# Splitting each modulation product around the column halves of its network product

## The chip, the cores and the metric

The kernel runs on one core of one Trainium2 chip. The time is device microseconds of one execution on that core. Three runs of the kernel before gave 2127.76, 2130.54 and 2132.85 us; the median is 2130.54 us.

## The reference

Two blocks of a model run one behind the other on 256 tokens of width 1024. The first block has two layers; each ends with a convolutional gated network (hidden width 2816):

```python
def conv_glu(x, w_in, conv_w, conv_b, w_out):
    gate, val = jnp.split(x @ w_in, 2, axis=-1)
    gate = lax.conv_general_dilated(gate, conv_w[:, None, :], ...) + conv_b   # 3 taps along the tokens
    return (jax.nn.gelu(gate, approximate=False) * val) @ w_out
```

The second block needs modulation vectors that do not depend on x:

```python
def ada_params(sc, w, b):          # sc: silu of the condition, w: 1024 x 6144, for each of two layers
    mod = sc @ w + b
    return [t[:, None, :] for t in jnp.split(mod, 6, axis=-1)]
```

The kernel computes layer 0's modulation product inside the first convolutional stage and layer 1's inside the second, because sc (two rows: context and latent) is known from the start. Everything else of the reference (attention, state-space mixer, conformer module, gated networks) lies outside the change.

## The kernel before

**Slabs.** All weights come as slabs of 128 x 2048 fp32 (1 MB), in one fixed order, into a ring of four places in SBUF. SyncE issues every load in that order, one queue, one behind the other. Before the load of slab g it waits for one of two things (L2235 to L2240 of `sync`): as a rule for the semaphore `slab_begun` to reach g - 2, which TensorE counts up when it begins a slab's product, so that the slab four places earlier is done with; for most network slabs of the convolutional stages it waits instead for `lo_ready`, since those slabs are no longer read once they are split.

**Splitting.** A network slab isn't multiplied as it lies in the ring. ScalarE copies it into `w_hi` (fp32r, `hi`, L2696, two halves of 128 x 1024), GpSimd writes the rest ring - w_hi as a second fp32r tile (`lo`, L2146, two halves). In the stages f0 and f1 the rest goes to the place of `w_hi` before its own, so that only two networks are held at a time: ScalarE may write network n+2 only once network n's product is done (`one_conv` waits for `full["dve"][u]` and then calls `ahead`). TensorE computes three matmuls for each of 8 row chunks and 2 column halves: w_hi by x_hi (L1664), rest by x_hi (L1666), w_hi by x_lo (L1668). That makes 48 matmuls for one network, 24 for a column half `ch`.

**The two stages.** f0 and f1 have 46 slabs each: modulation slab 0, network slab 0, modulation slab 1, network slab 1 and so on up to 21, and then modulation slabs 22 and 23. In program order TensorE does modulation product u (`ada`, L1885: 8 fp32 matmuls, each in the trace as two records; the output is 32 partitions wide, so four of them stand side by side in the 128 partitions of one bank, and the second four are summed onto the first), and then network product u (`col_T_split`). A loop of five rounds does four pairs each, two pairs follow, then the last two modulation products and the second product of the network (`rows_split`, L1718, eleven slabs "fo").

**Who frees what.** `begun` raises `slab_begun` by 2 on the first matmul of the network product: once for the modulation slab just used, once for the network slab. One further count was given just before the stage. So the load of modulation slab n+2, which takes the place of modulation slab n, goes out when network n begins, and network slab n+2 is the next one in SyncE's queue; its own wait, for the rest of network n, is over by then. The first two slabs of the second product, fo0 and fo1, go out in the same way when network 21 begins.

```python
# TensorE, network(layer)
with L.rounds(5, per | {("took", "lo_ready"): 8}) as i:
    for u in range(4):
        ada(stage, 2 * u, u, 2 * i)
        col_T_split(stage, 2 * u + 1, u, waits=turned if u == 0 else None)
# SyncE
for g in range(SLABS):
    if g in halves_read:
        sp.wait_ge(S["lo_ready"], halves_read[g])
    elif g >= RING:
        sp.wait_ge(S["slab_begun"], g - 2)
    sp.dma_start(ring[:, g % RING, :], slabs[SOURCE[g]]).then_inc(landed[g % RING], 16)
```

**Behind the products.** VectorE turns each modulation result (`turn_ada`, L2358) and then works on the network (`convolved`, L2338 to L2350), with ScalarE's gelu and copies in between. Two banks serve the modulation products, four the networks.

Of the kernel before, what the change touches and what calls it, by code (L numbers as in the profile page):

```python
# [34 lines left out]
KC = D // P  # L35
# [142 lines left out]
def build(nc, slabs, x_in, xT_in, memT_in, ctx_in, pt_in, row_in, ln_in, wdt_in, out):  # L178
    with ExitStack() as ctx:
# [113 lines left out]
        def part(name, at, *dims):  # L293
            return nc.alloc_sbuf_tensor_at(name, [P, *dims], F32R, offset=at)
# [3 lines left out]
        x_hi = part("x_hi", arena_at + 4 * 18432, KC, T)  # L298
        x_lo = part("x_lo", tri_at, KC, T)
# [1277 lines left out]
        def _(pe):  # L1577
# [3 lines left out]
            def free_of(b):  # L1581

                return free[last.get(b, "act")][b]

            def frees(b):

                return L.now((last.get(b, "act"), b))
# [3 lines left out]
            def fill(ins, b, first, then=None):  # L1591

                ins.then_inc(full[first][b], 1)
                if first == "dve":
                    filled_dve[b] += 1 if L.per is None else 5
                last[b] = then or first
                L.up((last[b], b))

            def for_rounds(reader):

                for b in range(4):
                    if last[b] != reader:
                        pe.wait_ge(free_of(b), frees(b))
                        last[b] = reader

            def slab(stage, u, i=0):

                g = FIRST[stage] + u
                pe.wait_ge(landed[g % RING], 16 * (g // RING + 1) + i * 16)
                return ring[:, g % RING, :]  # L1610

            def begun(ins, first, slabs=1):

                if first and slabs:
                    ins.then_inc(S["slab_begun"], slabs)
# [25 lines left out]
            def pair(stage, u):  # L1644

                pe.wait_ge(S["lo_ready"], L.took("lo_ready", 2))
                return (FIRST[stage] + u) % RING

            def col_T_half(stage, u, ch, b, src=(x_hi, x_lo), used_up=False, waits=None):

                if ch == 0:
                    pair(stage, u)
                    pe.wait_ge(free_of(b), frees(b))
                s = (FIRST[stage] + u) % RING
                wh = w_hi[:, s, :].rearrange("p (k c) -> p k c", k=KC)
                early = stage in ("f0", "f1")
                wl = (w_hi[:, (s - 1) % RING, :] if early else w_lo[:, s, :]) \
                    .rearrange("p (k c) -> p k c", k=KC)
                dst, c = bank[b][:, ch * T:(ch + 1) * T], slice(ch * P, (ch + 1) * P)
                for k in range(KC):  # L1660
                    if waits and ch == 0 and k in waits:
                        for sem, count in waits[k]:
                            pe.wait_ge(sem, count)
                    ins = pe.matmul(dst, wh[:, k, c], src[0][:, k, :], start=(k == 0), stop=False)  # L1664
                    begun(ins, ch == 0 and k == 0, 2 if early else 1)
                    ins = pe.matmul(dst, wl[:, k, c], src[0][:, k, :], start=False, stop=False)  # L1666
                    begun(ins, used_up and ch == 1 and k == KC - 1)
                    ins = pe.matmul(dst, wh[:, k, c], src[1][:, k, :], start=False,  # L1668
                                    stop=(k == KC - 1))
                if ch == 1:  # L1670
                    fill(ins, b, "dve" if early else "act")

            def col_T_split(stage, u, b, src=(x_hi, x_lo), used_up=False, waits=None):

                for ch in range(2):
                    col_T_half(stage, u, ch, b, src, used_up, waits)

            def turned_x():

                return {0: [(free_of(b), frees(b)) for b in (4, 6)],  # L1680
                        4: [(free_of(b), frees(b)) for b in (5, 7)]}
# [189 lines left out]
                        fill(ins, 4 + q, "act")  # L1871
                    marks["ctxT"] = {b: L.now(("act", b)) for b in range(8)}

            def ada(stage, u, r, i=0, last_one=False):

                w = slab(stage, u, i).rearrange("p (k c) -> p k c", k=KC)  # L1880
                b = 5 + r % 2
                pe.wait_ge(free_of(b), frees(b))
                for k in range(KC):
                    q = 32 * (k % 4)
                    ins = pe.matmul(bank[b][q:q + 32, 0:256], sc_in[:, k, :], w[:, k, :],  # L1885
                                    start=(k < 4), stop=(k >= 4))

                    begun(ins, k == 0 and last_one)
                fill(ins, b, "dve")

            def ada_columns(layer):

# [9 lines left out]
            def network(layer):  # L1902

                stage = f"f{layer}"
                if layer == 0:
                    pe.wait_ge(S["sc_ready"], L.took("sc_ready"))
                    pe.wait_ge(S["pick_ready"], L.took("pick_ready"))
                for_rounds("dve")
                marks[f"net{layer}"] = dict(filled_dve)
                marks[f"ada{layer}"] = {b: L.now(("dve", b)) for b in (0, 1, 2, 3, 5, 6)}  # L1910
                turned = turned_x()
                for b_ in (5, 6):
                    pe.wait_ge(free_of(b_), frees(b_))
                    last[b_] = "dve"
                per = {("dve", q): 1 for q in range(4)} | {("dve", q): 2 for q in (5, 6)}
                with L.rounds(5, per | {("took", "lo_ready"): 8}) as i:
                    for u in range(4):

                        ada(stage, 2 * u, u, 2 * i)
                        col_T_split(stage, 2 * u + 1, u, waits=turned if u == 0 else None)  # L1920
                for u in range(2):
                    ada(stage, 2 * u, u, 10)
                    col_T_split(stage, 2 * u + 41, u)
                ada(stage, 4, 2, 10)
                ada(stage, 5, 3, 10, last_one=True)
                def between(j):

                    if j == 2:
                        ada_columns(layer)
                    if layer:  # L1930
                        turn_ctx(j)
                rows_split(f"fo{layer}", hook=between)
# [25 lines left out]
            for h in range(DIFF_HEADS + 3):  # L1958
                if h < DIFF_HEADS:
                    for c in range(2):  # L1960
                        b = 4 + 2 * (h % 2) + c
                        pe.wait_ge(free_of(b), frees(b))
                    for tt in range(NT):
                        for c in range(2):
                            part = slice(c * HEAD, (c + 1) * HEAD)
                            ins = pe.matmul(bank[4 + 2 * (h % 2) + c][:, tt * T:(tt + 1) * T],
                                            qT[part, h, tt * P:(tt + 1) * P], kT[part, h, :],
                                            start=True, stop=True)
                            if tt:
                                fill(ins, 4 + 2 * (h % 2) + c, "dve")  # L1970
                if h >= 3:
# [3 lines left out]
                    for tt in range(NT):  # L1975
                        for kt in range(NT):
                            ins = pe.matmul(bank[2][:, tt * P:(tt + 1) * P],
                                            aT[:, g % 2, kt * T + tt * P:kt * T + (tt + 1) * P],
                                            vN[:, kt, g * P:(g + 1) * P],
                                            start=(kt == 0), stop=(kt == NT - 1))  # L1980
                    fill(ins, 2, "act")
                if 0 <= h - 2 < DIFF_HEADS:
# [3 lines left out]
                    for kt in range(NT):  # L1986
                        for tt in range(NT):
                            ins = pe.transpose(bank[g % 2][:, kt * T + tt * P:kt * T + (tt + 1) * P],
                                               aS[:, g % 3, tt * T + kt * P:tt * T + (kt + 1) * P],
                                               ident[:, :])  # L1990
                    fill(ins, g % 2, "act")
                if h < DIFF_HEADS:
                    col_T_half("xk0", h // 2, h % 2, 3, (m_hi, m_lo))
                else:
                    for g in (2 * (h - 8), 2 * (h - 8) + 1):
                        turn_head(g)
# [3 lines left out]
            cross(0)  # L2000
            while_norm("T", "xk1", used_up=True)
            network(0)
            tokens_to_T(by_class=True)
            turned = turned_x()
# [23 lines left out]
            for q in range(pairs + 3):  # L2028
                if q < pairs:
                    for tt in range(NT):  # L2030
# [3 lines left out]
                        for g, (at, n, cols) in enumerate([(0, T, slice(0, T)), (T, P, keys),  # L2034
                                                           (T + P, P, keys)]):
                            for hh in range(2):
                                part = slice(hh * HEAD, (hh + 1) * HEAD)
                                ins = pe.matmul(bank[2 * hh + tt][:, at:at + n],  # L2038
                                                gqT[part, 8 * g + q, tt * P:(tt + 1) * P],
                                                gkT[part, 8 * g + q, cols], start=True, stop=True)  # L2040
# [4 lines left out]
                if q >= 3:  # L2045
                    k = q - 3
                    b = 6 + k % 2
# [6 lines left out]
                    for n, (g, kt, cols) in enumerate(blocks):  # L2054
                        wide = cols.stop - cols.start
                        for hh in range(2):
                            col = g * D + (2 * k + hh) * HEAD
                            ins = pe.matmul(bank[b][hh * HEAD:(hh + 1) * HEAD, cols],
                                            gvN[:, kt, col:col + HEAD],
                                            gPT[:, 2 * (k % 2) + hh, at:at + wide],  # L2060
                                            start=(n == 0), stop=(n == 5))
# [932 lines left out]
```

## Time and profile before

| what | value |
|---|---|
| median of 3 runs | 2130.54 us |
| the profiled execution, its own time | 2126.64 us |
| span of the profiled execution | 2124.9 us |
| PE busy | 1931.2 us (91%) |
| POOL busy | 1258.8 us (59%) |
| DVE busy | 1083.8 us (51%) |
| ACT busy | 994.5 us (47%) |

The span is the profiled part of the one execution; the other 1.7 us of its time lie around it. PE is TensorE's matmuls, PEld its weight loads, DVE VectorE, ACT ScalarE, POOL GpSimd, SPq the queue of SyncE. Busy time of PE includes pipelining: a matmul of 256 columns has a record of about 0.28 us, but in a stream the next one starts 0.12 us later. So the start times say how fast a stream runs, and the busy share does not. The two convolutional stages lie at about 302 to 463 us and 940 to 1104 us of the span.

### The profile page before, as it was taken

The page shows a single profiled execution, that of the slowest core. Times are in us where ns is not written, and L with a number is a line of the kernel's source. Part 1 is how long each engine was busy: PE and PEld are TensorE (multiplying, and loading weights), DVE is VectorE, ACT ScalarE, POOL GpSimd, SP SyncE. Part 2 cuts the span into 40 slices and gives each one's busy share as a digit, 9 for nine tenths or more (in the row PEclk, how much of TensorE's full clock was granted, in tenths as well). Part 3 has the DMA queues.
Part 4 walks back from the last instruction along what each step waited for, and adds up shares of the span by engine and source line. Part 5 has one row for each costly group of instructions (what it writes and reads, how often), then busy time and mean ns, then how long its engine had stood idle before and what let it go on. Part 6 is the DMA issues. An engine that isn't in the chain of part 4 may idle for free.

```text
span 2124.9 us, 33890 instructions
## 1 busy us (share of the span) xinstructions
PE 1931.2 (91%) x13581; PEld 1704.6 (80%) x13581; DVE 1083.8 (51%) x1511; ACT 994.5 (47%) x1718; POOL 1258.8 (59%) x588
## 2 busy tenths in 40 slices
PE   6879989999899979989999889998879998978997
PEld 6868888877899966868877868876669987948996
DVE  7783146641100073136657655678767942846641
ACT  3453435443444373434554444478744546425542
POOL 9647566678688602646669334300468885426995
PEclk9999999999899999999999999999989998989999
DMA  6325367764555503357774212211235553314552
GB/s 251 139 93 186 112 224 293 302 259 175 177 181 190 187 1 139 119 220 279 298 274 161 80 62 97 99 60 64 86 135 182 181 194 121 119 61 164 182 192 104
DMA packets 48321, 342.30 MB, mean 161 GB/s; under 512 B 5264, under 2 KB 6288, under 8 KB 7248
## 3 DMA queue, kind: packets, MB, share of 16 engines
q1 hardware_dynamic: 45968, 328.22, 42.3%
q0 software_dynamic: 2240, 12.49, 1.5%
q8 instruction: 80, 1.31, 0.2%
q14 instruction: 33, 0.27, 0.0%
HBM read 339.65 MB, written 1.05 MB: 160 GB/s over the span
## 4 chain that ended last, share of the span: by engine, by line
PE 65%; DVE 17%; ACT 7%; POOL 5%; issue 5%; DMA 1%; DVEq 0%; POOLq 0%; SPq 0%; ACTq 0%
PE bank L1664 11%; PE bank L1668 11%; PE bank L1666 11%; PE bank L1718 11%; DVE arena L902 2%; POOL w_lo L2146 2%; PE bank L1762 2%; PE bank L1277 2%; POOL w_hi L2146 2%; PE bank L1279 2%; PE bank L1280 2%; PE bank L1699 2%; PE bank L1698 2%; PE bank L1696 2%; ACT arena L1102 2%
## 5 line engine op out<-in xcount | busy, mean ns | idle before, releaser
L2146 POOL TENSOR_TENSOR w_lo<-ring,w_hi 128x1024 fp32r<-128x1024 f32 x360 | 876.8, 2461 | 314.4 <-ACT w_hi L2696 313.9
L1664 PE MATMUL bank<-x_hi,w_hi 128*128 128x256 f32 x2176 | 615.7, 283 | 29.9 <-POOL w_lo L2146 16.6
L1668 PE MATMUL bank<-x_lo,w_hi 128*128 128x256 f32 x2176 | 618.4, 284 | 0.0
L2696 ACT ACTIVATE w_hi<-ring 128x1024 fp32r<-128x1024 f32 x448 | 448.7, 1052 | 348.8 <-DMA ring<-slabs_dram 344.7
L1664 PEld LDWEIGHTS bank<-x_hi,w_hi 128*128 128x128 f32 x2176 | 414.4, 190 | 50.5 <-issue 50.5
L1668 PEld LDWEIGHTS bank<-x_lo,w_hi 128*128 128x128 f32 x2176 | 413.6, 190 | 0.0
L1666 PE MATMUL bank<-x_hi,w_lo 128*128 128x256 f32 x1472 | 413.4, 281 | 0.0
L1666 PEld LDWEIGHTS bank<-x_hi,w_lo 128*128 128x128 f32 x1472 | 281.3, 191 | 0.0
L2146 POOL TENSOR_TENSOR w_hi<-ring,w_hi 128x1024 fp32r<-128x1024 f32 x88 | 208.8, 2394 | 110.9 <-ACT w_hi L2696 110.9
L2634 ACT ACTIVATE arena<-bank 128x512 f32<-128x512 f32 (+1 forms) x182 | 100.1, 563 | 296.9 <-PE bank L1668 190.8
L1666 PE MATMUL bank<-x_hi,w_hi 128*128 128x256 f32 x704 | 197.5, 281 | 0.0
L398 POOL TENSOR_TENSOR w_lo<-ring,w_half 128x1024 fp32r<-128x1024 f32 x32 | 77.7, 2433 | 112.3 <-ACT w_half L989 112.2
L1666 PEld LDWEIGHTS bank<-x_hi,w_hi 128*128 128x128 f32 x704 | 132.9, 189 | 0.0
L2594 DVE CUSTOM_DVE_ANT_0 arena<-bank,dist 128x512 f32<-128x512 f32 x32 | 22.1, 692 | 214.9 <-PE bank L2038 214.3
L1718 PE MATMUL bank<-w_hi,h_hi 128*128 128x512 f32 x352 | 112.9, 398 | 11.4 <-POOL w_lo L2146 9.8
L711 DVE SCALAR_TENSOR_TENSOR arena<-bank,pt,arena 128x508 f32<-128x508 f32 (+3 forms) x128 | 87.3, 682 | 60.0 <-ACT arena L1004 56.4
L1718 PE MATMUL bank<-w_lo,h_hi 128*128 128x512 f32 x352 | 112.1, 396 | 0.0
L1718 PE MATMUL bank<-w_hi,h_lo 128*128 128x512 f32 x352 | 111.9, 395 | 0.0
L1277 PE MATMUL bank<-s_hi,w_half 128*128 128x512 f32 (+1 forms) x288 | 104.6, 363 | 2.0 <-DVE s_lo L643 2.0
L2350 DVE TENSOR_TENSOR h_lo<-arena,h_hi 128x256 f32 (+1 forms) x44 | 85.2, 1936 | 33.3 <-ACT h_hi L2778 33.3
L1280 PE MATMUL bank<-s_hi,w_lo 128*128 128x512 f32 (+1 forms) x288 | 101.9, 354 | 0.0
L1279 PE MATMUL bank<-s_lo,w_half 128*128 128x512 f32 (+1 forms) x288 | 101.8, 353 | 0.0
(341 smaller groups left out, 3657.9 us busy)
## 6 DMA issues: line engine op xcount, KB each, us to landing
ring<-slabs_dram SPq DMA_DIRECT2D x312, 1024.0 KB, 4.8
lnrow<-ln_dram POOLq DMA_DIRECT2D x6, 1024.0 KB, 5.0
xt<-xT_dram SPq DMA_DIRECT2D x1, 1024.0 KB, 5.9
xt<-memT_dram POOLq DMA_DIRECT2D x1, 1024.0 KB, 14.0
x<-x_dram POOLq DMA_DIRECT2D x1, 1024.0 KB, 17.9
arena<-ctx_dram POOLq DMA_DIRECT2D x1, 1024.0 KB, 7.0
lnrow<-ln_dram POOLq DMA_DIRECT2D x2, 512.0 KB, 4.8
res<-x POOLq DMA_DIRECT2D x2, 512.0 KB, 3.2
```

What stands on the lines that cost most here:

```text
L711: ins = v.scalar_tensor_tensor(out=d3[:, :, lo:hi], in0=s3[:, :, lo + o:hi + o], scalar=pt[:, scw + k * 32 + j:scw + k * 32 + j + 1], in1= ...
L1277: ins = pe.matmul(dst, wh[:, k, :], hi_(k), start=(k == 0), stop=False)
L1279: pe.matmul(dst, wh[:, k, :], lo_(k), start=False, stop=False)
L1280: ins = pe.matmul(dst, wl[:, k, :], hi_(k), start=False, stop=(k == KC - 1))
L1664: ins = pe.matmul(dst, wh[:, k, c], src[0][:, k, :], start=(k == 0), stop=False)
L1666: ins = pe.matmul(dst, wl[:, k, c], src[0][:, k, :], start=False, stop=False)
L1668: ins = pe.matmul(dst, wh[:, k, c], src[1][:, k, :], start=False, stop=(k == KC - 1))
L1718: ins = pe.matmul(bank[2 * tt + h][:, :], st, w[:, k, h * 512:(h + 1) * 512], start=(first and n == 0), stop=(end and n == 2))
L2146: pool.tensor_tensor(dst[:, c], ring[:, s, c], w_hi[:, s, c].bitcast(F32), ALU.subtract).then_inc(S["lo_ready"], 1)
L2350: v.tensor_tensor(h_lo[:, j, :], act[:, u, :], h_hi[:, j, :].bitcast(F32), ALU.subtract).then_inc(S["hT_ready"], 1)
L2634: a.activation(dst, bank[b][:, :] if src is None else src, ACT.Copy if not kw else ACT.Identity, **kw).then_inc(free["act"][b], 1)
L2696: a.activation(w_hi[:, g % RING, c], ring[:, g % RING, c], ACT.Copy) \
```

## The change

Each pair of a modulation product and its network product becomes: four modulation matmuls (k = 0 to 3), the first column half of the network, the other four modulation matmuls (k = 4 to 7), the second column half. The modulation slab is then in use until the middle of the network, so the count of 2 on `slab_begun` moves from the first matmul of column half 0 to the first matmul of column half 1. All instructions stay; one wait on the landed slab is added for each pair. The last two modulation products stay whole.

```diff
@@ col_T_half
                     ins = pe.matmul(dst, wh[:, k, c], src[0][:, k, :], start=(k == 0), stop=False)
-                    begun(ins, ch == 0 and k == 0, 2 if early else 1)
+                    if early:
+                        begun(ins, ch == 1 and k == 0, 2)
+                    else:
+                        begun(ins, ch == 0 and k == 0)
@@ col_T_split
-            def col_T_split(stage, u, b, src=(x_hi, x_lo), used_up=False, waits=None):
+            def col_T_split(stage, u, b, src=(x_hi, x_lo), used_up=False, waits=None, between=None):
                 for ch in range(2):
+                    if ch and between:
+                        between()
                     col_T_half(stage, u, ch, b, src, used_up, waits)
@@ ada
-            def ada(stage, u, r, i=0, last_one=False):
+            def ada(stage, u, r, i=0, last_one=False, half=None):
                 w = slab(stage, u, i).rearrange("p (k c) -> p k c", k=KC)
                 b = 5 + r % 2
-                pe.wait_ge(free_of(b), frees(b))
-                for k in range(KC):
+                if half != 1:
+                    pe.wait_ge(free_of(b), frees(b))
+                for k in range(KC) if half is None else range(4 * half, 4 * half + 4):
                     q = 32 * (k % 4)
                     ins = pe.matmul(bank[b][q:q + 32, 0:256], sc_in[:, k, :], w[:, k, :],
                                     start=(k < 4), stop=(k >= 4))
                     begun(ins, k == 0 and last_one)
-                fill(ins, b, "dve")
+                if half != 0:
+                    fill(ins, b, "dve")
+
+            def ada_and_net(stage, j, u, i=0, waits=None):
+                ada(stage, 2 * j, u, i, half=0)
+                col_T_split(stage, 2 * j + 1, u, waits=waits,
+                            between=lambda: ada(stage, 2 * j, u, i, half=1))
@@ network
                     for u in range(4):
-                        ada(stage, 2 * u, u, 2 * i)
-                        col_T_split(stage, 2 * u + 1, u, waits=turned if u == 0 else None)
+                        ada_and_net(stage, u, u, 2 * i, turned if u == 0 else None)
                 for u in range(2):
-                    ada(stage, 2 * u, u, 10)
-                    col_T_split(stage, 2 * u + 41, u)
+                    ada_and_net(stage, 20 + u, u)
```

## Rows read from the trace of the kernel before

**Rows 1.** Page: the span, and TensorE's busy time, share and instructions.

```profile
span 2124.9 us, 33890 instructions
PE 1931.2 (91%) x13581; PEld 1704.6 (80%) x13581; DVE 1083.8 (51%) x1511; ACT 994.5 (47%) x1718; POOL 1258.8 (59%) x588
```

**Rows 2.** Windows, network 1 to 21, both stages: span, PE, PEld, DVE, ACT, POOL, PEclk, DMA, GB/s.

```profile
311.87:450.53 138.66, 137.37 (x1280) 122.71 (x1281) 88.49 (x116) 69.29 (x109) 95.00 (x40) 1.00 0.79 303
949.45:1092.16 142.71, 137.48 (x1285) 122.74 (x1281) 87.03 (x118) 69.90 (x110) 94.86 (x40) 1.00 0.77 298
```

**Rows 3.** Waits, 300 to 460 us: us in total, times, longest.

```profile
ACT w_hi L2696 <- DMA ring<-slabs_dram: 52.7, 21, 4.2
POOL w_hi L2146 <- ACT w_hi L2696: 50.2, 21, 6.5
```

**Rows 4.** Waits of SyncE's queue, 300 to 460 us.

```profile
SPq L2240 <- PE bank L1664: 131.7, 22, 7.6
```

**Rows 5.** Timeline, network 11 and its successors: start, us, engine, line [idle before <-releaser].

```profile
380.29 0.28 PE L1668 MATMUL bank<-x_lo,w_hi 128*128 128x256 f32 x1
380.50 1.07 PE L1885 MATMUL bank<-ring,sc_in 128*32 128x256 f32 x16
381.54 0.19 PEld L1664 LDWEIGHTS bank<-x_hi,w_hi 128*128 128x128 f32 x1 [0.45 <-issue]
381.57 0.36 PE L1664 MATMUL bank<-x_hi,w_hi 128*128 128x256 f32 x1
...
381.95 0.33 SPq L2240 DMA_DIRECT2D ring<-slabs_dram  x1
382.32 0.43 SPq L2240 DMA_DIRECT2D ring<-slabs_dram  x1
...
387.18 0.28 PE L1668 MATMUL bank<-x_lo,w_hi 128*128 128x256 f32 x1
...
389.26 2.01 ACT L2696 ACTIVATE w_hi<-ring 128x1024 fp32r<-128x1024 f32 x2 [3.41 <-DMA ring<-slabs_dram]
390.40 4.74 POOL L2146 TENSOR_TENSOR w_hi<-ring,w_hi 128x1024 fp32r<-128x1024 f32 x2 [2.21 <-ACT w_hi L2696]
...
395.37 0.38 PE L1664 MATMUL bank<-x_hi,w_hi 128*128 128x256 f32 x1
```

**Rows 6.** The tile sc_in: records of the modulation products, ns min/median/max.

```profile
L1885 PE MATMUL bank<-ring,sc_in x768: 379/379/637, 302.4 to 1099.6; 128*32 128x256 f32 x192
```

**Rows 7.** Line L2240, the loads issued at 381.95 and at 382.32 us.

```profile
DMA to landing us min/median/max: 4.8/4.8/4.8
...
DMA to landing us min/median/max: 6.9/6.9/6.9
```

**Rows 8.** Timeline, first stage: start of network 1, of network 21, and fo0's way to TensorE.

```profile
311.87 0.36 PE L1664 MATMUL bank<-x_hi,w_hi 128*128 128x256 f32 x1 [1.56 <-issue]
...
450.53 0.36 PE L1664 MATMUL bank<-x_hi,w_hi 128*128 128x256 f32 x1
...
456.47 2.01 ACT L2696 ACTIVATE w_hi<-ring 128x1024 fp32r<-128x1024 f32 x2 [1.99 <-PE bank L1668]
...
462.63 0.76 PE L1718 MATMUL bank<-w_hi,h_hi 128*128 128x512 f32 x1 [4.33 <-POOL w_lo L2146]
```

**Rows 9.** Timeline, second stage: network 0, network 2's copy, starts of networks 2, 3, 21.

```profile
941.97 0.58 PE L1664 MATMUL bank<-x_hi,w_hi 128*128 128x256 f32 x1
...
952.81 2.01 ACT L2696 ACTIVATE w_hi<-ring 128x1024 fp32r<-128x1024 f32 x2 [2.90 <-DMA ring<-slabs_dram]
...
958.89 0.36 PE L1664 MATMUL bank<-x_hi,w_hi 128*128 128x256 f32 x1 [2.51 <-POOL w_hi L2146]
...
965.71 0.39 PE L1664 MATMUL bank<-x_hi,w_hi 128*128 128x256 f32 x1
...
1092.15 0.39 PE L1664 MATMUL bank<-x_hi,w_hi 128*128 128x256 f32 x1
```

**Rows 10.** Windows of two waits of TensorE, columns as in rows 2.

```profile
956.00:958.00 2.00, 0.37 (x8) 0.00 (x0) 0.58 (x2) 1.27 (x5) 2.00 (x2) 1.00 0.25 102
...
462.00:464.00 2.00, 1.37 (x3) 1.16 (x4) 0.00 (x0) 2.00 (x3) 1.96 (x2) 0.53 0.01 4
```

## The prediction

> **What bounds the kernel now.** I read the page first, then the two stages that the change touches by windows, then their waits, and last the timeline of one pair. On the page [rows 1] TensorE is busy for 91% of the span; the reader is to see from it only that a delay of TensorE will seldom be hidden. It doesn't say what paces the stages. The windows [rows 2] take twenty pairs each: 138.66 us in the first stage, 142.71 us in the second, so 6.93 and 7.14 us for one pair, with the granted clock at 1.00. The waits [rows 3] show a second pace beside TensorE's: ScalarE waits 52.7 us in 21 places for a slab to land, and GpSimd 50.2 us for ScalarE. SyncE itself waits 131.7 us, 22 times, for the first matmul of a network, L1664 [rows 4]. So the loads aren't ahead of their use; each goes out on a signal from TensorE.
>
> The timeline of one pair [rows 5] puts both paces side by side. TensorE alone: the last matmul of network 10 starts at 380.29, the block of 16 modulation records at 380.50, network 11 at 381.57, its last matmul at 387.18. That is 1.28 us across the block, then 5.61 us for 47 steps, 0.119 us each: 6.9 us for a pair. The chain of one slab: network 11 begins at 381.57; its signal lets the load of modulation slab 13 go at 381.95 and that of network slab 13 at 382.32, 0.75 us after the start. ScalarE starts on it at 389.26, 6.94 us after the issue; the landing times, 4.8 us for the first of the two loads and 6.9 us for the second, agree [rows 7]. GpSimd starts at 390.40 (1.14 us more) and needs 4.74 us, to 395.14. Network 13 begins at 395.37, 0.23 us later. The sum is 0.75 + 6.94 + 1.14 + 4.74 + 0.23 = 13.8 us for two pairs, exactly two times 6.9. TensorE's own work and the way from its signal back to it are equal here. Whatever makes the signal later, by d, adds d to every second pair, with no slack in between.
>
> **The change, part by part.** Removed: nothing. *The mid-network half.* The block of eight matmuls is four groups of four; the whole takes 1.07 us and one record 0.38 us [rows 5, 6], so the groups follow at (1.07 - 0.38) / 3 = 0.23 us. Across a whole block I read 1.28 us from matmul to matmul; across half of one I take 1.28 - 2 x 0.23 = 0.82 us, which assumes that entering (0.21 us) and leaving (0.45 us from the last modulation weights to the first network weights, rows 5) cost the same as now. The trace has no such half block. From below its cost is the two groups alone, 0.46 us (plus one step of 0.12), from above the whole block, 1.28 us. I take 0.82, because the gaps on either side belong to the change of shape and stay whole for a half. TensorE's own work for a pair becomes 46 x 0.119 + 2 x 0.82 = 7.1 us, 0.2 us more than now.
>
> The row shows weights of the network waiting 0.45 us behind the modulation records [rows 5]. The Trainium skill ("TensorEngine Tiling (Array Packing)", Tiling Modes, Key Properties) says that changing the tiling mode drains the engine; by that rule the change pays two drains more for each pair, which is the 0.82 taken here, and the row agrees. Another of its pages ("TensorE: Matmul & The Clock Gate", Part 3) has TensorE pull weight loads ahead of running matmuls where groups differ; by that one the half would cost 0.46 us and the total below would be some 8 us less. The row speaks against it.
>
> *The moved signal.* It moves from the first matmul of column half 0 to that of column half 1: 23 steps of 0.119 and the half block, 2.74 + 0.82 = 3.6 us after the start of the network. Both loads move with it. The modulation slab waits for the signal itself, and the network slab is queued behind it on SyncE, though its own condition (the rest of network n is written) has long been met. Behind them come ScalarE's copy, and behind that in ScalarE's order the gelu, and GpSimd's rest; TensorE waits for the last. The chain for two pairs is now 13.8 + 3.6 = 17.4 us, 8.7 us a pair, against 7.1 us of TensorE's work. The cover that hid the load until now, the second and first halves of two networks, is used up, and TensorE will stand still for 1.6 us in each pair.
>
> *The rest* costs nothing: the wait on a landed slab in the middle is for a slab already in use; half a block less in front of the network falls into TensorE's new wait for GpSimd; VectorE turns a modulation result later, but its bank is asked for again two pairs on; VectorE's and ScalarE's work for one network (88.49 and 69.29 us in 20 pairs, rows 2) fits into 8.7 us; network 1's own slab is loaded before the first moved signal.
>
> *First stage.* From network 1 [rows 8] to 21 are ten double steps: 10 x 17.4 = 174.0 instead of 450.53 - 311.87 = 138.66 us: +35.4. Then fo0, the first slab of the next product, is issued on network 21's signal. Now it has landed when network 21 ends, and ScalarE starts on it at 456.47, 5.94 us after the start of network 21. After, it is issued at 3.6 + 0.38 and lands 4.8 us later, at 8.8 us, and ScalarE takes it up at about 8.9: +3.0. From fo0 on TensorE paces the product, and the shift stays. Together +38.4 us.
>
> *Second stage.* The chain of the even networks begins at 941.97, on the slow clock and with a slow load: ScalarE gets network slab 2 at 952.81 [rows 9], where 0.75 + 6.94 would give 949.7. That excess is other traffic, which runs out meanwhile. After, I place the second issue near 947.0 and the landing at 954.0; so network 2 begins at about 960.1 (958.89 now), and network 3, whose load follows network 1's signal, at 967.1 (965.71 now): +1.4. From 3 to 21 are nine double steps: 967.1 + 9 x 17.4 = 1123.7 against 1092.15: +31.5. With +3.0 for fo0: +34.5 us.
>
> The sum is +73 us on the profiled execution's 2126.64 us: 2199.6 us. The median of the runs stands 3.9 us, or 0.2%, above that execution, so I predict 2203.5 us, 3.4% more.
>
> **The rivals.** *(A) The load is hidden anyway,* and only TensorE's changes of shape count. For it: the DMA engines are only busy 0.79 of the time [rows 2]. Against it: ScalarE already waits for the landing in 21 of 22 networks [rows 3], and the chain adds up to the whole double step. It would give 0.2 us x 44 pairs = +9 (up to 0.5 x 44 = +20 with the half at its dearest), about 2140 to 2150 us.
>
> *(B) The clock falls too.* TensorE now stands still in each pair. At 462 to 464, behind a wait of 4.3 us [rows 8], the granted clock was 0.53 [rows 10]. If each first column half ran at 1.2 GHz, its 23 steps and the half block would take some 2.7 us more in the chain (256 columns at 1.2 GHz are 0.213 us, against 0.119), 1.35 us a pair: +54 us on top with the tails, about 2258 us. Against it: around 956 to 958, with 0.37 us of matmuls in the 2 us and TensorE's next start only at 958.89, the clock stayed at 1.00 [rows 9, 10], and the new waits are shorter.
>
> *(C) Not slower: the half slips under the network's matmuls.* If four narrow matmuls in the middle cost one group's pitch and no change of shape (0.23 + 0.12 us, twice a pair), TensorE's pair would be 46 x 0.119 + 0.7 = 6.2 us, 0.7 us under today's, and with the landing free of the signal up to 44 x 0.7 = 31 us would be gained, 2100 us. It decides only from where the chain gets below 13.8 us. Even at 0.35 us the signal is 3.1 us later, so the landing would have to come 3.8 us after the issue, and the shortest in the rows is 4.8 us, for the first of the two loads [rows 7]. I see nothing that speaks for this.
>
> **How the numbers follow.** The forecast gets 0.8, (A) 0.07, (B) 0.08, (C) 0.03, and 0.02 remain for something else. The forecast's own range: the half block at 0.46 or 1.28 us moves nineteen double steps and two tails by -0.36 or +0.46 each, -8 or +10 us; the landing and the start behind GpSimd scatter by 0.1 to 0.2 us a step, 3 us; the second stage's beginning is open by some 3 us. That gives 2191 to 2217 us. To hold 8 in 10 the range has to be wider than that toward both neighbours, without reaching them: 2184 to 2232 us. A difference under 0.2% can't be told from none here. Slower by more than that hold the forecast, (A) and (B): 0.95 or so; faster 0.03, same 0.02.
>
> **What would show it.** In the changed kernel a double step between networks should be 17.4 us; the issues of SyncE 3.9 us behind the start of a network instead of 0.38; ScalarE's wait for the landing in each pair up from 2.5 us on average to about 5 us; TensorE's wait on GpSimd (L2146) near 1.6 us in each pair, 60 to 70 us in all; the landing still 6.9 us behind the issue; the clock still 1.00 in both stages; nothing moved outside them but the two tails. A double step near 14.3 us would make (A) right; a granted clock under 1.00 in the first halves, (B). The forecast is wrong if the signal isn't what the loads wait for, or if the landing gets shorter than 6 us when it is alone.

## The result, and the profile after

The changed kernel takes 2227.54 us (median of 4 runs, 2222.74 to 2232.32), the kernel before 2129.15 us in the same comparison: ratio 1.0467, 95% interval 1.045 to 1.0483. It is slower by 98 us; the forecast was slower by 73 us, and the range (to 2232 us) holds the time. The profiled execution of the changed kernel took 2229.16 us.

The page of the changed kernel, the lines that answer to [rows 1], and the clock by slices:

```profile
span 2227.4 us, 33875 instructions
PE 1976.5 (89%) x13581; PEld 1730.8 (78%) x13581; DVE 1044.0 (47%) x1511; ACT 993.7 (45%) x1718; POOL 1255.3 (56%) x588
...
PEclk9999999999899999988999999999998999989999
```

The number of matmuls is the same, and the busy time of ScalarE and GpSimd too. The span grew by 102.5 us and TensorE's busy time by 45 us. Windows of the changed kernel, networks 1 to 21 of both stages, columns as in [rows 2]:

```profile
311.79:496.16 184.37, 153.62 (x1281) 130.14 (x1281) 88.76 (x117) 68.97 (x109) 94.19 (x40) 0.94 0.60 232
1001.85:1191.05 189.20, 160.36 (x1285) 136.29 (x1281) 90.78 (x121) 69.71 (x110) 94.17 (x40) 0.90 0.57 222
```

184.37 us against 138.66 us and 189.20 against 142.71 [rows 2]. The reader is to see two things: the DMA engines fell from 0.79 to 0.60 busy, so nothing new competes with the loads, they only start later, and the granted clock is 0.94 and 0.90, where it was 1.00. (While the loads of a pair run, the engines are full all the same: 0.96 to 1.01 at 392 to 394 and at 398 to 402, in the windows below.) From the start of network 0 in the second stage (941.97 us before, 993.53 us after) to fo0's product (1104.27 and 1206.07 us) the growth is 50.2 us; the first stage with its tail, to 462.63 and 513.38 us, grew by 50.8 us. All the rest of the kernel has 1.5 us more. The forecast had +34.5 us for the second stage and +38.4 us for the first.

Waits of the changed kernel in the first stage, 300 to 510 us, the lines that answer to [rows 3] and [rows 4] and the new one of TensorE:

```profile
ACT w_hi L2703 <- DMA ring<-slabs_dram: 113.5, 22, 9.9
POOL w_hi L2153 <- ACT w_hi L2703: 97.9, 21, 8.7
...
PE bank L1664 <- POOL w_hi L2153: 32.1, 12, 4.2
```

```profile
SPq L2247 <- PE bank L1664: 183.6, 22, 12.8
```

The timeline of the changed kernel around networks 6, 7 and 8, columns as in [rows 5], and the landing of the two loads issued there, as in [rows 7]:

```profile
356.29 0.39 PE L1664 MATMUL bank<-x_hi,w_hi 128*128 128x256 f32 x1
...
359.32 0.64 PE L1887 MATMUL bank<-ring,sc_in 128*32 128x256 f32 x8
359.89 0.19 PEld L1664 LDWEIGHTS bank<-x_hi,w_hi 128*128 128x128 f32 x1 [0.41 <-issue]
359.89 0.39 PE L1664 MATMUL bank<-x_hi,w_hi 128*128 128x256 f32 x1
...
360.11 0.28 PE L1669 MATMUL bank<-x_hi,w_hi 128*128 128x256 f32 x1
...
360.31 0.80 SPq L2247 DMA_DIRECT2D ring<-slabs_dram  x2
...
366.33 0.39 PE L1664 MATMUL bank<-x_hi,w_hi 128*128 128x256 f32 x1 [2.77 <-POOL w_hi L2153]
...
367.51 2.01 ACT L2703 ACTIVATE w_hi<-ring 128x1024 fp32r<-128x1024 f32 x2 [3.69 <-DMA ring<-slabs_dram]
...
373.62 0.35 PE L1664 MATMUL bank<-x_hi,w_hi 128*128 128x256 f32 x1
```

```profile
L2247 SPq DMA_DIRECT2D ring<-slabs_dram x2: 327/380/432, 360.3 to 360.7; - x2
...
DMA to landing us min/median/max: 4.7/5.8/6.8
```

Network 6 starts at 356.29, its column half 1 at 359.89: 3.60 us, as forecast. The loads go out at 360.31, ScalarE starts at 367.51, network 8 at 373.62: 17.3 us for the double step (from a network's start to that of the next but one), where 17.4 was forecast. So far every term holds. But the networks aren't evenly spaced. Network 7 starts 10.04 us after network 6, behind a wait of 2.77 us, and network 8 only 7.29 us after network 7. Two networks further on, in front of network 9, such a wait has a second effect (networks 9, 10 and 11, columns as in [rows 5], then the windows):

```profile
383.55 0.39 PE L1664 MATMUL bank<-x_hi,w_hi 128*128 128x256 f32 x1 [2.71 <-POOL w_hi L2153]
...
388.66 0.38 PE L1664 MATMUL bank<-x_hi,w_hi 128*128 128x256 f32 x1
...
391.47 0.28 PE L1671 MATMUL bank<-x_lo,w_hi 128*128 128x256 f32 x1
391.68 0.64 PE L1887 MATMUL bank<-ring,sc_in 128*32 128x256 f32 x8
392.25 0.39 PE L1664 MATMUL bank<-x_hi,w_hi 128*128 128x256 f32 x1
...
398.67 0.28 PE L1671 MATMUL bank<-x_lo,w_hi 128*128 128x256 f32 x1
398.88 0.64 PE L1887 MATMUL bank<-ring,sc_in 128*32 128x256 f32 x8
402.31 0.58 PE L1664 MATMUL bank<-x_hi,w_hi 128*128 128x256 f32 x1 [2.79 <-POOL w_hi L2153]
```

```profile
384.00:386.00 2.00, 2.00 (x16) 2.00 (x15) 1.18 (x3) 1.03 (x2) 0.00 (x0) 0.77 0.07 29
386.00:388.00 2.00, 2.00 (x13) 1.73 (x16) 0.78 (x2) 1.98 (x3) 1.90 (x1) 0.50 0.00 0
388.00:390.00 2.00, 2.00 (x19) 1.34 (x12) 0.43 (x2) 1.21 (x4) 2.00 (x2) 0.88 0.00 0
...
392.00:394.00 2.00, 2.00 (x22) 1.75 (x15) 1.51 (x3) 0.00 (x0) 0.00 (x0) 1.00 1.01 426
...
398.00:400.00 2.00, 1.51 (x16) 0.90 (x15) 0.42 (x1) 1.26 (x4) 2.00 (x2) 1.00 0.96 406
400.00:402.00 2.00, 0.00 (x0) 0.00 (x0) 1.97 (x1) 0.00 (x0) 2.00 (x1) 1.00 0.99 418
402.00:404.00 2.00, 1.69 (x8) 1.70 (x9) 1.53 (x3) 0.46 (x1) 0.25 (x1) 0.53 0.42 176
```

Behind the wait TensorE is on 1.2 GHz for part of the network (granted 0.50 and 0.53 of 2.4 GHz). Network 9's first half takes 5.11 us (383.55 to 388.66) instead of 3.60. So network 10, which comes behind it, starts 1.5 us later, and so does the signal for network 11. Since both are late by the same time, the wait in front of network 11 is as long as before, 2.79 us, and the clock is slow again. The median double step over the trace is 18.65 us in the first stage and 18.85 us in the second; 18 of 44 networks contain slow clock, and one of them, network 0 of the second stage, has it in every kernel here.

### The profile page after: what moved, and what is told of

Its sections match the earlier page's. It is cut to its first block, busy times and chain, and to the rows that moved or that the text cites. A ratio compares the mean times of both kernels' runs of the same rounds, so it can differ in the third digit from the quotient of the medians.

```text
span 2227.4 us, 33875 instructions
## 1 busy us (share of the span) xinstructions
PE 1976.5 (89%) x13581; PEld 1730.8 (78%) x13581; DVE 1044.0 (47%) x1511; ACT 993.7 (45%) x1718; POOL 1255.3 (56%) x588
## 4 chain that ended last, share of the span: by engine, by line
PE 53%; DVE 15%; issue 13%; POOL 10%; ACT 7%; DMA 2%; POOLq 0%; DVEq 0%; SPq 0%; ACTq 0%
PE bank L1723 11%; PE bank L1671 8%; PE bank L1664 8%; PE bank L1669 8%; POOL w_hi L2153 6%; POOL w_lo L2153 3%; DMA ring<-slabs_dram 2%; DVE arena L902 2%; PE bank L1767 2%; PE bank L1277 2%; PE bank L1279 2%; PE bank L1280 2%; PE bank L1704 2%; PE bank L1703 2%; PE bank L1701 2%
## 5 line engine op out<-in xcount | busy, mean ns | idle before, releaser
L1664 PE MATMUL bank<-x_hi,w_hi 128*128 128x256 f32 x2176 | 633.6, 291 | 83.5 <-POOL w_hi L2153 61.0
L1671 PE MATMUL bank<-x_lo,w_hi 128*128 128x256 f32 x2176 | 629.9, 289 | 0.0
L1664 PEld LDWEIGHTS bank<-x_hi,w_hi 128*128 128x128 f32 x2176 | 426.1, 196 | 124.6 <-issue 82.0
L1671 PEld LDWEIGHTS bank<-x_lo,w_hi 128*128 128x128 f32 x2176 | 426.1, 196 | 0.0
L1669 PE MATMUL bank<-x_hi,w_hi 128*128 128x256 f32 x704 | 209.4, 297 | 0.0
L1669 PEld LDWEIGHTS bank<-x_hi,w_hi 128*128 128x128 f32 x704 | 145.3, 206 | 0.0
L1723 PE MATMUL bank<-w_hi,h_hi 128*128 128x512 f32 x352 | 113.6, 400 | 15.7 <-POOL w_lo L2153 14.1
L2334 DVE TENSOR_TENSOR h_lo<-arena,h_hi 128x256 f32 (+1 forms) x44 | 101.5, 2306 | 5.0
L2357 DVE TENSOR_TENSOR h_lo<-arena,h_hi 128x256 f32 (+1 forms) x44 | 87.9, 1997 | 33.3 <-ACT h_hi L2785 33.3
## 6 DMA issues: line engine op xcount, KB each, us to landing
x<-x_dram POOLq DMA_DIRECT2D x1, 1024.0 KB, 17.8
```

Source lines behind the costliest of these rows:

```text
L1723: ins = pe.matmul(bank[2 * tt + h][:, :], st, w[:, k, h * 512:(h + 1) * 512], start=(first and n == 0), stop=(end and n == 2))
L2334: v.tensor_tensor(h_lo[:, j, :], act[:, u, :], h_hi[:, j, :].bitcast(F32), ALU.subtract).then_inc(S["hT_ready"], 1)
L2357: v.tensor_tensor(h_lo[:, j, :], act[:, u, :], h_hi[:, j, :].bitcast(F32), ALU.subtract).then_inc(S["hT_ready"], 1)
```

## The experiments

### Only the signal is moved

The modulation product is whole and in front, as before:

```diff
-                    begun(ins, ch == 0 and k == 0, 2 if early else 1)
+                    begun(ins, (ch == 1 and k == 0) if early else (ch == 0 and k == 0), 2 if early else 1)
```

> The kernel before with one edit: the signal that frees the slabs moves to the first matmul of column half 1; the modulation product stays whole, in front. Theory (the moved signal lengthens a chain with no slack): the signal is 24 matmuls later, 2.9 us, so a double step is 13.8 + 2.9 = 16.7 us; ten of them in the first stage and nine in the second give +28 and +24 us, the two tails +2.3 each, together +57 us (ratio 1.027) while the clock stays at 2.4 GHz. Where the granted clock falls behind the wait, up to 1.5 us more for a double step, up to +85 us (1.040). Rival (the split blocks on TensorE are the cost): no split here, so ratio 1.00.

Measured: 2211.27 us, ratio 1.039 (1.0356 to 1.0424). Nothing is split here, and four fifths of the loss are there, 81 of 98 us. The median double step is 17.8 us in the first stage and 17.9 us in the second, the shortest 16.3 us. The windows of networks 1 to 21 show the slow clock again:

```profile
311.34:488.24 176.90, 147.65 (x1281) 132.41 (x1281) 88.35 (x116) 69.23 (x109) 94.23 (x40) 0.93 0.63 241
993.34:1172.38 179.04, 151.96 (x1284) 137.09 (x1281) 90.58 (x120) 69.33 (x110) 94.22 (x40) 0.90 0.60 235
```

The rival, the split blocks, falls as a main cause.

### The signal is moved by half as much

```diff
+                    begun(ins, (ch == 0 and k == 4) if early else (ch == 0 and k == 0), 2 if early else 1)
```

> The same, with the signal on the matmul of row chunk 4 in column half 0: 12 matmuls later, 1.45 us. Theory: a double step of 15.2 us, +14 and +11 us in the stages, +0.7 for each tail, together +26 us (ratio 1.012), and the clock stays at 1.00, since TensorE then waits for only 0.7 us in a pair. If there were slack in the chain, less than half of that. Rival (split blocks are the cost): 1.00.

Measured: 2157.41 us, ratio 1.014 (1.0105 to 1.0175). The double step is 15.2 us in the median of both stages, as expected, and in the first stage the clock stays:

```profile
312.55:466.18 153.63, 138.18 (x1280) 122.73 (x1281) 87.94 (x116) 68.99 (x109) 94.69 (x40) 1.00 0.71 274
```

In the second stage it doesn't quite: network 4 starts behind a wait of only 1.80 us and meets the slow clock once. That costs about 1.5 us.

```profile
989.78 0.36 PE L1664 MATMUL bank<-x_hi,w_hi 128*128 128x256 f32 x1 [1.80 <-POOL w_hi L2146]
```

```profile
990.00:992.00 2.00, 2.00 (x11) 2.00 (x11) 1.50 (x4) 1.82 (x2) 0.68 (x1) 0.52 0.00 0
```

1.45 us on the signal gave 153.63 - 138.66 = 15.0 us in ten double steps. Each microsecond of the signal is a microsecond of every second network, from the first on. There is no slack.

### Spare work in TensorE's wait

The changed kernel, with ten matmuls behind each network product that the reference doesn't need:

```diff
                             between=lambda: ada(stage, 2 * j, u, i, half=1))
+                for _ in range(10):
+                    pe.matmul(bank[7][:, 0:T], x_hi[:, 0, 0:P], x_hi[:, 0, :], start=True, stop=True)
```

> The changed kernel with ten spare matmuls (128x256, into a bank that nobody reads, 1.2 us) behind each network product of the two stages, in the time in which TensorE waits for GpSimd. They are work that the reference does not need. Theory (the part of the loss beyond the forecast is TensorE's clock falling to 1.2 GHz in every second network, because the wait in front of it is 3 to 4 us long): the clock stays at 1.00 in both stages, every double step is 17.3 us, and the kernel is faster by some 25 us than the changed one: ratio about 1.034 instead of 1.047. Rival (TensorE's own work or its drains make the excess): 44 times 1.2 us are added, ratio about 1.07.

Measured: 2201.18 us, ratio 1.0343 (1.0313 to 1.0373). With 440 matmuls more the kernel is 26 us faster than the changed one. The clock is 1.00 over both stretches, network 1 to 21, and the median double step 17.4 us in each:

```profile
312.86:487.11 174.25, 168.62 (x1481) 145.75 (x1481) 89.38 (x116) 68.85 (x109) 94.92 (x40) 1.00 0.62 241
988.71:1162.23 173.52, 168.22 (x1484) 145.70 (x1480) 89.62 (x117) 68.88 (x109) 94.97 (x40) 1.00 0.62 242
```

This is the kernel that I had forecast: 174.25 us where the prediction has 174.0, and +71 us in all where it has +73. The other 26 us of the changed kernel are the clock. Its own trace agrees: 17 of its networks 1 to 21 met the slow clock, and their first halves took 26.9 us more in sum than at 3.60 us each. The spare work does two things, and this run doesn't part them: it fills the gap with full-width matmuls, and it cuts what is left of the wait to 1.2 us at most (11.5 us in all, with 61 us in the changed kernel).

### The loads of each pair are swapped in the queue

The changed kernel; SyncE's loop runs over this order:

```diff
-            for g in range(SLABS):
+            order = list(range(SLABS))
+            for layer in range(2):
+                for n in range(2, FC):
+                    g = FIRST[f"f{layer}"] + 2 * n
+                    order[g], order[g + 1] = g + 1, g
+            for g in order:
```

> The changed kernel with the loads of each pair swapped in SyncE's order in both stages: network slab n+2 first, which waits only for the rest of network n, then modulation slab n+2, which waits for the signal in the middle of network n. The network slab then isn't held by the signal of its own pair but by that of the pair before, 3.6 us before the start of network n+1. Theory (the queue behind the signal is the cost): the chain is off the path, TensorE paces the stages at 7.2 us a pair: 20 x 7.2 = 144 us against 139 and 143 us before, plus 3 us for each tail: about +12 us, ratio 1.006. Rival (the split itself, or slower landings, are the cost): the ratio stays above 1.03.

Measured: 2142.25 us, ratio 1.0062 (1.0044 to 1.008), the expected number. The split products and the late signal are all still there; only the network slab no longer stands behind the signal of its own pair. It isn't the landing that got faster: from network 4 on most network slabs land 6.4 to 7.5 us behind their issue (6.9 us before), some 4.7 to 5.8 us, and TensorE waits behind neither. Its windows show a TensorE that never pauses, at 7.19 us a pair:

```profile
315.09:458.95 143.86, 143.86 (x1280) 122.04 (x1280) 85.04 (x119) 69.91 (x109) 95.00 (x40) 1.00 0.77 282
960.93:1104.79 143.86, 143.86 (x1284) 122.04 (x1280) 85.99 (x121) 71.40 (x110) 95.00 (x40) 1.00 0.79 284
```

Its waits from 300 to 470 us show what ScalarE now waits for, TensorE and hardly any landing:

```profile
ACT w_hi L2708 <- PE bank L1671: 40.1, 15, 3.7
...
ACT w_hi L2708 <- DMA ring<-slabs_dram: 10.2, 2, 6.1
```

### The same order for the kernel before

> The kernel before, modulation products whole and the signal where it was, with the loads of each pair swapped in SyncE's order (network slab first), as in the run before. Theory: the chain of the loads leaves the path, and TensorE alone paces the stages at 6.87 us a pair, 137 us for twenty against 138.7 and 142.7 before; tails unchanged. About 7 us less, ratio 0.997. It also gives the price of the split alone, against 143.9 us with it: 0.3 us a pair. Rival (the chain has slack in the kernel before): 1.000.

Measured: 2121.63 us, ratio 0.9957 (0.9943 to 0.9971), against 2131.49 us for the kernel before in the same comparison. The swap alone makes the kernel before 10 us (0.4%) faster, 7 us was expected; it makes the two stages equal, 1.6 and 5.6 us shorter from network 1 to 21:

```profile
312.22:449.26 137.04, 137.04 (x1281) 122.61 (x1281) 84.35 (x119) 69.56 (x109) 95.48 (x40) 1.00 0.80 306
947.79:1084.85 137.06, 137.06 (x1284) 122.78 (x1280) 83.95 (x121) 70.95 (x110) 95.03 (x40) 1.00 0.79 300
```

It also gives the price of the split with nothing else in play: 143.86 - 137.05 = 6.8 us for twenty pairs, 0.34 us for each.

### Spare work with the whole product and the late signal

The first experiment with eight spare matmuls behind each network product.

> The whole modulation products with the signal on column half 1 (ratio 1.039 so far), and eight spare matmuls behind each network product. Theory (clock): no fall of the granted clock in the stages, every double step at the shortest seen without the spare work, 16.4 us, so 164 us for twenty pairs in place of 177 and 179; ratio about 1.025. Rival: 44 times 1 us are added, 1.06.

Measured: 2185.02 us, ratio 1.0266 (1.0246 to 1.0286), 26 us under the first experiment. The clock is at 1.00, the median double step 16.6 us:

```profile
312.75:479.85 167.10, 157.03 (x1440) 141.67 (x1441) 89.28 (x116) 68.90 (x109) 94.75 (x40) 1.00 0.65 252
980.09:1146.03 165.94, 156.75 (x1444) 141.69 (x1441) 89.40 (x117) 68.87 (x109) 94.78 (x40) 1.00 0.66 253
```

The clock's part is the same with and without the split.

## Why the prediction was right, and where it fell short

**The two equal paces** of the kernel before: right. A signal about 1.45 us later gave 15.0 us in ten double steps, and taking the load out of the queue behind the signal took nearly all of the loss away.

**The moved signal and the network slab queued behind it:** right, and sized right. 3.60 us, and 17.3 us for a double step without slow clock. The second load of the pair is issued 0.37 us behind the first and lands 6.8 us later, where ScalarE starts, at 367.51: the landing got no shorter. ScalarE's wait for it is 113.5 us in 22 places, 5.2 us each, where about 5 was forecast. TensorE's wait for GpSimd is 32.1 us in the first stage and 28.8 us in the second, 61 us in all, where 60 to 70 was forecast.

**The half block:** taken at 0.82 us. In the changed kernel the step across one is 392.25 - 391.47 = 0.78 us. That is close to the value taken and well above the 0.46 us of the groups alone, so the gaps at the change of shape do stay whole. The rule on drains in the Trainium skill ("TensorEngine Tiling (Array Packing)", Tiling Modes, Key Properties) agrees with this row. The prediction's other citation didn't bear on the case: the page of the Trainium skill "TensorE: Matmul & The Clock Gate", Part 3, speaks of differing row groups, and here both shapes take all 128 rows (`128*32` and `128*128`). The 0.46 us worked out beside it did not come.

The split's price for TensorE was put at 0.2 us a pair and is 0.34. The term left out is the step behind a block, from the network's first matmul to its second. It is 0.22 us (359.89 to 360.11) where the other steps are 0.12, and a pair now has it twice.

**The tails:** +3.0 us each was forecast. In the kernel with spare work, where the clock stays up, network 21 to fo0's product takes 15.08 and 15.09 us, 3.0 us more than before. In the changed kernel the first stage has 17.2 us, because network 21 itself met the slow clock, and the second 15.0 us.

**What fell short is rival (B), given 0.08 and set aside.** The step that failed is "Against it: [...] and the new waits are shorter". The forecast spread the waiting evenly, 1.6 us in each pair. The sum was right (61 us); the trace has it in every second pair: spacings of 10.0 and 7.3 us at networks 6 to 8, later 10.1 and 8.7 us. So the long waits are mostly 2.7 to 3.1 us, longer than the 2.51 us that had left the clock at 1.00 [rows 9, 10]. With the half block of narrow matmuls before it, the one in front of network 11 makes 3.6 us from one network's last matmul (398.67) to the next one's first (402.31). The even and the odd networks are two chains, each paced by its own loads; nothing centres one between the other. The price of (B) was also off, the other way: 1.5 us for a double step that it touches, not 2.7, because the clock is back before the first half is over (network 9's half ends at 388.66, and 388 to 390 already has 0.88). Forecast (73) and clock (26) give 99 us; measured are 98. By stages: the first has 12.4 us beyond its forecast, 11.2 of them in slow first halves and the rest in network 3's load, which landed 8.1 us after its issue, 1.2 us later than the others; the second 15.7 us, and 15.8 in slow first halves. That the slow clock costs these 26 us is shown by both runs with spare work. Two things stay open. One is why the first long wait comes where it does: the wait in front of network 3, behind that late load, is the first that brought the slow clock, but no run takes that landing alone away. The other is which waits bring the slow clock: their length doesn't decide it alone (see the last section).

**Rival (A)** would have been right only for a kernel whose loads don't stand behind the signal; the swapped order is that kernel, and it has +12 us where (A) had +9 to +20. (The upper figure was mis-sized: 0.5 x 44 is 22, and with the half block at 1.28 us, TensorE's pair would be 1.1 us longer, some 50 us in all.) **Rival (C)** had nothing for it and has nothing now.

## What to carry to other kernels

Before a signal that frees a buffer is moved, follow it round: signal, issue, landing, each engine that prepares the data, and back to the engine that gave the signal; if the sum is equal to the period, every nanosecond is paid. In an in-order queue look also at what stands behind the waiting load: here it was the second load that cost, and its own condition had long been met, so the cheapest cure was the order of two loads. And a wait that a forecast spreads evenly may come in lumps when two chains alternate; on TensorE the lump can also take the clock.

## What the runs showed of the hardware that wasn't expected

TensorE's granted clock fell to 0.50 behind waits for GpSimd, and the length of the wait didn't decide it. In the changed kernel, networks 1 to 21, it fell in 17 networks, behind waits of 2.5 to 4.2 us, and not in networks 5, 7 and 17 of the first stage, which started behind 2.89, 2.77 and 2.76 us. With the signal moved by half as much it fell once, behind 1.80 us. With only the signal moved it stayed at 1.00 behind the 2.91 us in front of this network:

```profile
1094.35 0.36 PE L1664 MATMUL bank<-x_hi,w_hi 128*128 128x256 f32 x1 [2.91 <-POOL w_hi L2146]
```

```profile
1094.00:1096.00 2.00, 1.66 (x14) 1.69 (x15) 1.62 (x4) 0.93 (x1) 0.11 (x1) 1.00 0.17 70
1096.00:1098.00 2.00, 2.00 (x20) 2.00 (x19) 1.14 (x3) 1.49 (x4) 1.79 (x1) 1.00 0.00 0
```

What decides it stays open. Ten spare matmuls of 256 columns behind each network kept the clock at 1.00 from network 1 to 21 of both stages, and the kernel with more work was faster by 26 us.
